# Second attention of a two-block kernel: the order of a step on TensorE and on VectorE

## The chip, the cores and the metric

The kernel runs on one core of one Trainium2 chip. The metric is the device time of one execution in microseconds (us). Before the change the median of three runs is 907.81 us (907.81 to 908.78). One further execution was profiled: 908.62 us, of which the profile's span, from the first instruction to the last, is 906.8 us.

## The reference, cut to what matters

The program computes a two-layer transformer block (a first attention layer, an MLP, a second attention layer, an MLP) and then a differential-attention layer, for 256 tokens of width 1024. Only the second attention layer bears on the change, and of it the two branches that attend over tokens. With 256 tokens all four 64-token blocks are kept and the window of 512 covers every earlier token, so both are causal softmax attentions over the same 256 keys, each with its own keys and values:

```python
s_s = jnp.einsum('bqghd,bgqkd->bghqk', qb, k_g) * scale
p_s = masked_softmax(s_s, valid_s[:, :, None]).astype(v_g.dtype)
o_s = jnp.einsum('bghqk,bgqkd->bqghd', p_s, v_g)
...
s_w = jnp.einsum('bqghd,bkgd->bghqk', qb, kw) * scale
p_w = masked_softmax(s_w, valid_w).astype(vw.dtype)
o_w = jnp.einsum('bghqk,bkgd->bqghd', p_w, vw)
out = gb[..., 0:1] * o_c + gb[..., 1:2] * o_s + gb[..., 2:3] * o_w
```

There are 16 heads in two groups of eight that share keys and values. The third branch (`o_c`, over 15 compressed keys) is computed for all heads at once, beside the steps described below.

## The kernel before

The kernel is written engine by engine: each engine has its own list of instructions, and counting semaphores order them. An engine does its list strictly in order, so an instruction that waits holds everything behind it on that engine.

The second attention is a software pipeline of 16 steps, one per head, counted by `it` from 0 to 18 (`STEPS_C = 16`, and `DEEP = 3` more to drain it). A step number `st` in the code is the head plus 8, since the eight steps of the first attention share the semaphores. For one head `n` the work is this, with the engine and the line that the profile shows:

- **Scores**, TensorE (`c_scores`, L1175): queries times both branches' keys. Token tile 0 goes to a bank of `pair`, tile 1 to a bank of `acc`; each has two banks, used by even and odd heads.
- **Maxima**, VectorE (`peaks`, L2000): four instructions add the causal mask, write the masked scores from PSUM to a buffer of `probs` in SBUF and leave the row maximum in `nb`. `probs` has three buffers (`DEEP`), so head `n` overwrites the buffer of head `n - 3`.
- **Exponentials**, ScalarE (`exponentials`, L1481): in place in `probs`, with the row sums. GpSimd makes of the sums the factors `cf` (L1893, L1913).
- **Two turns**, TensorE (`turn_p`, L974): turn 0 transposes the three 128x128 blocks of the first branch into the PSUM bank `ptp`, turn 1 those of the second branch into the same bank.
- **Two copies** out of `ptp`: the first on ScalarE (`p_first`, L1469), the second on VectorE (`p_second`, L2030).
- **Values**, TensorE (`mix`, L444): the transposed weights times the values, into `misc`. The program has six matmuls here; the trace shows each as two.
- **Scaling**, VectorE (`scaled`, L2036): `misc` times `cf` into `hr`; GpSimd adds the two branches into `o_tok` (L1918).

In iteration `it` the engines work on different heads: scores and maxima on head `it`, exponentials on head `it - 1`, the turns and copies on head `it - 3`, values and scaling on head `it - 4`. Before the change the order of an iteration is, for `it` from 4 to 15:

- TensorE: turn 0 of `it - 3`, scores of `it`, turn 1 of `it - 3`, values of `it - 4`.
- VectorE: copy of `it - 3`, maxima of `it`, scaling of `it - 4`. (For `it = 15` the maxima stand last.)
- ScalarE: copy of `it - 3`, exponentials of `it - 1`. This list is the same after the change.

The waits between them:

```python
def turn_p(st, a):                            # TensorE
    pe.wait_ge(s_exped, 2 * st + a + 1)
    pe.wait_ge(s_copied, 2 * st + a)
def mix(st, v):                               # TensorE
    pe.wait_ge(s_copied, 2 * st + 2)
    pe.wait_ge(s_scaled, st)
def peaks(st):                                # VectorE
    dve.wait_ge(s_turned, 2 * (st - DEEP + 1))
    dve.wait_ge(s_scored, 2 * st + t + 1)
```

Each turn adds one to `s_turned`, each copy one to `s_copied`. So a turn waits for the copy of the turn in front of it (one bank), the values of a head wait for its second copy, and the maxima of head `it` wait for turn 1 of head `it - 3`, whose buffer they overwrite.

Some iterations carry more, between the pieces named: on TensorE the scores against the compressed keys (`compressed_scores`, L1186 and L1191, at 3, 4, 7, 8), turns of query blocks (L417, at 3 and 5), a turn of the compressed weights (L1229, at 14); from 16 on the first turns of the output (`turn_outputs`, L1239 and L1243). On VectorE a weight split (L463, at 5, 8, 14), low halves of queries (L2278, at 4 and 6) and the softmax of the compressed branch (L2404 to L2417, from 7 to 13).

Of the kernel before, what the change touches and what calls it, by code (L numbers as in the profile page):

```python
# [90 lines left out]
def left(g):  # L91

    return g - min(max(g - G_ABO, 0), 2) - min(max(g - G_CO, 0), 2)
# [10 lines left out]
DEEP = 3  # L104
# [100 lines left out]
def program(nc, x, stream, consts_d, cols_d, rows_d, sel_d, out):  # L205
    with ExitStack() as ctx:  # L206
# [232 lines left out]
        def pe_pv(dst, src, v, w):  # L439

            for t, k0, nk in TK:
                for s in range(nk // P):
                    a = k0 + s * P
                    last = nc.tensor.matmul(dst[:, t * w:(t + 1) * w], src[:, a:a + P], v(s),  # L444
                                            start=s == 0, stop=s == nk // P - 1, skip_group_check=True)
            return last
# [231 lines left out]
        STEPS_AB = A_HEADS // 2 + B_HEADS // 2  # L678
        FOX = B_HEADS // 2
        STEPS_C = C_HEADS  # L680
# [3 lines left out]
        def c_q(st, n=1):  # L684

            tile, at_ = ((xh, KD + 4), (xl, KD + 4), (xh, 0), (xh, 4))[st // 4]
            return tile[:, at_ + st % 4:at_ + st % 4 + n, :]

        def c_keys(g, part):

            return (xh, xl)[part][:, KD + 2 * g:KD + 2 * g + 2, :]
# [9 lines left out]
        def c_q_bank(z):  # L701

            return (pair[Z_C % 2], pair[(Z_C + 1) % 2], acc[3], acc[3])[z]
# [15 lines left out]
        def c_bank(st, t):  # L719

            return (pair, acc)[t][st % 2][:, 0:2 * (t + 1) * P]

        def c_pt(st, a):

            return (pt, pt2)[st % 2][:, a, :]
# [48 lines left out]
        def _(pe):  # L774
# [193 lines left out]
            def turn_p(st, a):  # L968

                pe.wait_ge(s_exped, 2 * st + a + 1)  # L970
                pe.wait_ge(s_copied, 2 * st + a)
                pb = probs[:, st % DEEP, :]
                for k, c0 in enumerate((a * P, 2 * P + a * SEQ, 3 * P + a * SEQ)):
                    last = nc.tensor.transpose(ptp[:, k * P:(k + 1) * P], pb[:, c0:c0 + P], ident)  # L974
                last.then_inc(s_turned, 1)

            def mix(st, v):

                pe.wait_ge(s_copied, 2 * st + 2)
                if st >= 1:  # L980
                    pe.wait_ge(s_scaled, st)
                for a in range(2):
                    last = pe_pv(misc[:, a * P:(a + 1) * P], c_pt(st, a), v(a), HD)
                last.then_inc(s_mixed, 1)
# [182 lines left out]
            def c_scores(n):  # L1167

                st = STEPS_AB + n
                if st >= 2:  # L1170
                    pe.wait_ge(s_peaked, 2 * (st - 1))
                banks = [c_bank(st, t).rearrange("p (a k) -> p a k", a=2) for t in range(T)]
                for t in range(T):
                    for part in range(2):
                        last = mm(banks[t], c_q(n)[:, 0, t * P:(t + 1) * P], c_keys(n % CG, part)[:, :, 0:(t + 1) * P],  # L1175
                                  start=part == 0, stop=part == 1, skip_group_check=True)
                    last.then_inc(s_scored, 1)

            def c_values(n):

                return lambda a: lambda s: Y[:, s, (CVS, CVW)[a] + HD * (n % CG):(CVS, CVW)[a] + HD * (n % CG + 1)]
# [13 lines left out]

            def c_iter(it):

                if 0 <= it - DEEP < STEPS_C:
                    turn_p(STEPS_AB + it - DEEP, 0)
                if it < STEPS_C:  # L1200
                    c_scores(it)
                if it == 8:
                    compressed_scores(range(12, 16))
                if it >= STEPS_C:
                    mix(STEPS_AB + it - DEEP - 1, c_values(it - DEEP - 1))
                if 0 <= it - DEEP < STEPS_C:
                    turn_p(STEPS_AB + it - DEEP, 1)
                if DEEP < it < STEPS_C:
                    mix(STEPS_AB + it - DEEP - 1, c_values(it - DEEP - 1))
                if it == 3:  # L1210
                    pe.wait_ge(dve_prep, 10)
                    pe.wait_ge(ev_act, left(G_CO))
                    pe.wait_ge(ev_dve, left(G_CO))
                    compressed_scores(range(0, 4))
                if it == 4:
                    compressed_scores(range(4, 8))
                if it == 7:
                    pe.wait_ge(q_lo, 12)
                    compressed_scores(range(8, 12))
                if it in (3, 5):  # L1220
                    z = (it + 1) // 2
                    pe.wait_ge(q_roped, 6)
                    if z == 3:
                        pe.wait_ge(q_lo, 10)
                    pe_turn_z(pe, Z_C + z + 1, c_blocks[2 * z + 2:2 * z + 4], c_q_bank(z))
                if it == 14:
                    pe.wait_ge(dve_prep, 11)
                    for k in range(4):
                        last = nc.tensor.transpose(acc[3][:, k * P:(k + 1) * P], pc[:, k * P:(k + 1) * P], ident)  # L1229
                    last.then_inc(pe_prep, 1)  # L1230
# [739 lines left out]
        def _(dve):  # L1970
# [32 lines left out]
            def peaks(st):  # L2003

                dve.wait_ge(s_turned, 2 * (st - DEEP + 1))
                for t in range(T):
                    dve.wait_ge(s_scored, 2 * st + t + 1)
                    n = (t + 1) * P
                    for a in range(2):
                        last = masked_peak(st, a, t, c_bank(st, t)[:, a * n:(a + 1) * n], caus)  # L2010
                    last.then_inc(s_peaked, 1)
# [13 lines left out]
            def p_second(st):  # L2025

                dve.wait_ge(s_turned, 2 * st + 2)
                if st >= 2:
                    dve.wait_ge(s_mixed, st - 1)
                v_.tensor_copy(c_pt(st, 1), ptp[:, 0:KEYS]).then_inc(s_copied, 1)  # L2030
# [345 lines left out]
            def c_scaled(st):  # L2376

                if st >= 2:
                    dve.wait_ge(c_added, st - 1)
                scaled(STEPS_AB + st, c_mix(st), cf)  # L2380

            for it in range(STEPS_C + DEEP):
                if 0 <= it - DEEP < STEPS_C:
                    p_second(STEPS_AB + it - DEEP)
                if it < STEPS_C - 1:
                    peaks(STEPS_AB + it)
                if it > DEEP:
                    c_scaled(it - DEEP - 1)
                if it == STEPS_C - 1:
                    peaks(STEPS_AB + it)  # L2390
                if it in CO_SPLITS:
                    split(U_CO + CO_SPLITS.index(it))
                if it in (STEPS_C, STEPS_C + 1):
                    dve_turn_block(dve, 4, ccs=(it - STEPS_C,))
                if it == 1:
                    evac(dve, G_C + 3, U_CQ2 + 4, 1, Y[:, 1, CQ + GW:CQ + 2 * GW], rr(N_A1), GW)
                if it in (4, 6):
                    q_low(it // 2, Z_C + it // 2 + 1, 4 + it)
                if it in (7, 9):
                    b = it // 9  # L2400
                    dve.wait_ge(cmp_scored, b + 1)
                    parts = acc[2 + b][:, :].rearrange("p (t h a n) -> p t h n a", t=T, h=HPG, a=2)
                    for t in range(T):
                        v_.tensor_reduce(pc5[:, t, b], parts[:, t], AX.X, ALU.add).then_inc(parts_added, 1)  # L2404
                if it == 10:
                    dve.wait_ge(parts_added, 2 * T)
                    ch.link(v_.tensor_reduce(cmx, pcall, AX.X, ALU.max))
                    ch.link(v_.tensor_scalar(cmx, cmx, FLOOR, None, ALU.max))
                    v_.tensor_tensor(pcall, pcall, over_keys, ALU.subtract).then_inc(dve_mid, 1)
                if it == 12:  # L2410
                    dve.wait_ge(act_prep, 5)
                    ch.link(v_.tensor_reduce(cmx, pcall, AX.X, ALU.add))
                    ch.link(v_.tensor_scalar(cmx, cmx, 1e-30, None, ALU.max))
                if it == 13:
                    ch.link(v_.reciprocal(cmx, cmx))
                    ch.link(v_.tensor_tensor(cm3, cm3, gate_t[:, :, 0, :], ALU.mult))
                    v_.tensor_tensor(pcall, pcall, over_keys, ALU.mult).then_inc(dve_prep, 1)  # L2417
                if it == 15:
                    dve.wait_ge(pe_prep, 5)
                    v_.tensor_copy(pct[:, :], acc[3][:, :]).then_inc(dve_prep, 1)  # L2420
# [273 lines left out]
```

## Time and profile before

| | us |
|---|---|
| median of three runs | 907.81 (907.81 to 908.78) |
| the profiled execution, its own time | 908.62 |
| its span | 906.8 |
| TensorE busy | 890.7 (98%) |
| VectorE busy | 645.2 (71%) |
| ScalarE busy | 510.1 (56%) |
| GpSimd busy | 124.5 (14%) |

The second attention's steps lie between 369.9 and 433 us of the span, where the first scores and the last values are. Times in the rows below are microseconds from the span's start. PE is TensorE, PEld its weight loads, DVE VectorE, ACT ScalarE, POOL GpSimd. In a timeline a row is a group of equal instructions: its start, the time from the first one's start to the last one's end, engine, line, operation, output and input, and in brackets how long the engine stood idle before it and what released it. Matmuls overlap, so the next group may start before a row's time is over; what a group takes on the engine is read from start to start.

### The profile page before, as it was taken

How to read it: one execution, taken by the hardware profiler on the slowest of the kernel's cores; microseconds unless marked ns; L12 is line 12 of the kernel's file. 1: busy time of each engine (PE TensorE's matmuls, PEld its weight loads, DVE VectorE, ACT ScalarE, POOL GpSimd, SP SyncE). 2: the span in 40 equal slices, each digit the busy share in tenths (PEclk: the TensorE clock that was granted, in tenths of full speed). 3: DMA queues.
4: the chain of work that ended last, by engine and by line, in shares of the span. 5: the costliest groups of instructions: out<-in, count | busy, mean ns of one | idle time of the engine just before them, and what ended most of it. 6: DMA issues, size and time to landing. Idle time of an engine off the chain costs nothing. (4 is left out here: it accounts for less than half of the span.)

```text
span 906.8 us, 14857 instructions
## 1 busy us (share of the span) xinstructions
PE 890.7 (98%) x4796; PEld 745.2 (82%) x4796; DVE 645.2 (71%) x1305; ACT 510.1 (56%) x1017; POOL 124.5 (14%) x168
## 2 busy tenths in 40 slices
PE   8999999999999999999999999999999999999998
PEld 7878787888888888888878888888887778878876
DVE  4768756766666679687467666666876878777775
ACT  6654835444454466586354454444656666666573
POOL 1310300000000000354010000000430401400401
PEclk9999999999999999999999999999999999999999
DMA  9643143655555557010436565555464445454431
GB/s 343 225 158 98 46 144 123 210 198 191 191 194 193 190 178 247 33 47 25 140 116 217 196 192 192 195 191 188 141 223 145 140 140 182 147 182 141 162 117 47
DMA packets 41609, 145.75 MB, mean 161 GB/s; under 512 B 4688, under 2 KB 6224, under 8 KB 41552
## 3 DMA queue, kind: packets, MB, share of 16 engines
q1 hardware_dynamic: 41264, 144.93, 48.4%
q8 instruction: 34, 0.56, 0.3%
q14 instruction: 23, 0.19, 0.1%
q10 hardware_dynamic: 288, 0.07, 0.0%
HBM read 143.93 MB, written 1.05 MB: 160 GB/s over the span
## 5 line engine op out<-in xcount | busy, mean ns | idle before, releaser
L463 DVE TENSOR_TENSOR wl<-raw,wh 128x1024 fp32r<-128x1024 f32 (+2 forms) x270 | 329.1, 1222 | 88.7 <-ACT wh L458 86.2
L458 ACT ACTIVATE wh<-raw 128x1024 fp32r<-128x1024 f32 (+2 forms) x270 | 281.6, 1046 | 64.9 <-PE acc L355 43.4
L353 PE MATMUL acc<-wh,xhl 128*128 128x512 f32 (+1 forms) x472 | 190.7, 404 | 0.6 <-DVE xhl L2490 0.4
L355 PE MATMUL acc<-wh,xhl 128*128 128x512 f32 (+1 forms) x472 | 184.4, 391 | 0.0
L354 PE MATMUL acc<-wl,xhl 128*128 128x512 f32 (+1 forms) x472 | 183.9, 390 | 0.0
L353 PEld LDWEIGHTS acc<-wh,xhl 128*128 128x128 f32 x472 | 88.7, 188 | 25.0 <-issue 8.0
L355 PEld LDWEIGHTS acc<-wh,xhl 128*128 128x128 f32 x472 | 88.6, 188 | 19.2
L354 PEld LDWEIGHTS acc<-wl,xhl 128*128 128x128 f32 x472 | 88.8, 188 | 16.3
L353 PE MATMUL acc<-wh,hh 128*128 128x512 f32 x256 | 100.2, 391 | 0.0
L354 PE MATMUL acc<-wl,hh 128*128 128x512 f32 x256 | 100.0, 391 | 0.0
L355 PE MATMUL acc<-wh,hl 128*128 128x512 f32 x256 | 99.6, 389 | 0.0
L1507 ACT ACTIVATE hh<-hq 128x256 fp32r<-128x256 f32 x64 | 26.7, 418 | 77.3 <-PE acc L355 72.5
L815 PE MATMUL ptp<-xhl,wh 128*128 128x512 f32 x256 | 64.1, 390 | 1.1 <-DVE hr L2062 1.1
L1501 ACT ACTIVATE probs<-ptp 128x256 f32<-128x256 f32 x32 | 12.3, 383 | 93.7 <-PE ptp L822 93.7
L815 PE MATMUL misc<-xhl,wh 128*128 128x512 f32 x256 | 64.3, 391 | 0.7 <-DVE hr L2062 0.7
L2062 DVE TENSOR_TENSOR hr<-ptp,probs 128x256 f32<-128x256 f32 x32 | 13.6, 424 | 67.5 <-ACT probs L1501 67.5
L507 POOL TENSOR_SCALAR st<-st 128x2 f32<-128x2 f32 x7 | 2.4, 338 | 430.8 <-ACT o_tok L500 258.2
L815 PEld LDWEIGHTS misc<-xhl,wh 128*128 128x128 f32 x256 | 47.8, 188 | 11.2 <-DVE wl L463 1.5
L815 PEld LDWEIGHTS ptp<-xhl,wh 128*128 128x128 f32 x256 | 47.8, 188 | 11.2 <-issue 1.4
L355 PEld LDWEIGHTS acc<-wh,hl 128*128 128x128 f32 x256 | 48.1, 188 | 10.2
L353 PEld LDWEIGHTS acc<-wh,hh 128*128 128x128 f32 x256 | 48.2, 188 | 9.3
L354 PEld LDWEIGHTS acc<-wl,hh 128*128 128x128 f32 x256 | 48.2, 188 | 8.7
(302 smaller groups left out, 1355.2 us busy)
## 6 DMA issues: line engine op xcount, KB each, us to landing
raw<-stream SPq DMA_DIRECT2D x266, 512.0 KB, 3.4
raw<-stream SPq DMA_DIRECT2D x4, 352.0 KB, 5.7
h<-x SPq DMA_DIRECT2D x4, 256.0 KB, 4.0
out<-h SPq DMA_DIRECT2D x3, 256.0 KB, 2.1
row<-rows SPq DMA_DIRECT2D x1, 700.0 KB, 8.8
probs<-sel SPq DMA_DIRECT2D x1, 512.0 KB, 7.7
cst<-consts SPq DMA_DIRECT2D x1, 507.0 KB, 7.1
out<-h SPq DMA_DIRECT2D x2, 128.0 KB, 2.0
```

The source lines that it names most:

```text
L353: nc.tensor.matmul(out_, ah, bh, start=start, stop=False, skip_group_check=True)
L354: nc.tensor.matmul(out_, ah, bl, start=False, stop=False, skip_group_check=True)
L355: return nc.tensor.matmul(out_, al, bh, start=False, stop=stop_, skip_group_check=True)
L458: nc.scalar.activation(used(u, wh[:, u % SPLIT, :]), used(u, raw[:, u % RAW, :]), ACT.Copy).then_inc(w_hi, 1)
L463: nc.vector.tensor_tensor(used(u, wl[:, u % SPLIT, :]), used(u, raw[:, u % RAW, :]), used(u, wh[:, u % SPLIT, :]).bitcast(F32), ALU.subtra ...
L507: chain_link(nc.gpsimd.tensor_scalar(dst, src, 1.0 / width, EPS, ALU.mult, ALU.add))
L815: nc.tensor.matmul((ptp, misc)[f % 2][:, :], wh[:, u % SPLIT, k * P:(k + 1) * P], xhl[:, KD + k, :, :].rearrange("p a s -> p (a s)"), star ...
L1501: s_.activation(probs[:, f % 2, 0:SEQ], (ptp, misc)[f % 2][:, SEQ:2 * SEQ], ACT.Copy).then_inc(z_cross, 1)
L1507: s_.activation(hh[:, f % 2, :], hq[:, f % 2, :], ACT.Copy).then_inc(hid_hi, 1)
L2062: v_.tensor_tensor(hr[:, f % 2, :], bank[:, 0:SEQ], probs[:, f % 2, 0:SEQ], ALU.add).then_inc(z_summed, 1)
```

## The change

On TensorE the order of an iteration becomes scores of `it`, turn 0 of `it - 3`, values of `it - 4`, turn 1 of `it - 3`. On VectorE it becomes maxima of `it`, scaling of `it - 4`, copy of `it - 3`. No instruction is added or removed, and every wait stays on its instruction.

```diff
@@ c_iter(it), TensorE
-                if 0 <= it - DEEP < STEPS_C:
-                    turn_p(STEPS_AB + it - DEEP, 0)
+                if it == DEEP:
+                    turn_p(STEPS_AB, 0)
                 if it < STEPS_C:
                     c_scores(it)
+                if DEEP < it < STEPS_C + DEEP:
+                    turn_p(STEPS_AB + it - DEEP, 0)
                 if it == 8:
                     compressed_scores(range(12, 16))
-                if it >= STEPS_C:
+                if it > DEEP:
                     mix(STEPS_AB + it - DEEP - 1, c_values(it - DEEP - 1))
                 if 0 <= it - DEEP < STEPS_C:
                     turn_p(STEPS_AB + it - DEEP, 1)
-                if DEEP < it < STEPS_C:
-                    mix(STEPS_AB + it - DEEP - 1, c_values(it - DEEP - 1))
@@ loop over it, VectorE
-                if 0 <= it - DEEP < STEPS_C:
-                    p_second(STEPS_AB + it - DEEP)
-                if it < STEPS_C - 1:
+                if it < STEPS_C:
                     peaks(STEPS_AB + it)
                 if it > DEEP:
                     c_scaled(it - DEEP - 1)
-                if it == STEPS_C - 1:
-                    peaks(STEPS_AB + it)
+                if 0 <= it - DEEP < STEPS_C:
+                    p_second(STEPS_AB + it - DEEP)
```

TensorE, iteration 6, before the change (the semaphores that an instruction waits on stand in brackets; the rows without brackets are the rest of the same group):

```order
L974 MATMUL ptp<-cst,probs 128x128 [waits s_copied,s_exped]
L974 MATMUL ptp<-cst,probs 128x128 x2
L1175 MATMUL pair<-xhl 128x256 [waits s_peaked]
L1175 MATMUL pair<-xhl 128x256
L1175 MATMUL acc<-xhl 128x512 x2
L974 MATMUL ptp<-cst,probs 128x128 [waits s_copied,s_exped]
L974 MATMUL ptp<-cst,probs 128x128 x2
L444 MATMUL misc<-Y,pt 128x64 [waits s_scaled,s_copied]
L444 MATMUL misc<-Y,pt 128x64 x5
```

The same iteration after the change:

```order
L1175 MATMUL pair<-xhl 128x256 [waits s_peaked]
L1175 MATMUL pair<-xhl 128x256
L1175 MATMUL acc<-xhl 128x512 x2
L974 MATMUL ptp<-cst,probs 128x128 [waits s_copied,s_exped]
L974 MATMUL ptp<-cst,probs 128x128 x2
L444 MATMUL misc<-Y,pt 128x64 [waits s_scaled,s_copied]
L444 MATMUL misc<-Y,pt 128x64 x5
L974 MATMUL ptp<-cst,probs 128x128 [waits s_copied,s_exped]
L974 MATMUL ptp<-cst,probs 128x128 x2
```

The values have moved between the two turns, and the scores, which stood between them, in front. Between turn 1 of one iteration and turn 0 of the next there stood the values; now the scores stand there.

VectorE, iteration 10, before the change (the second instruction of each maximum, which stores `nb`, is listed by itself):

```order
L2030 COPY pt2<-ptp 128x384 [waits s_mixed,s_turned]
L2000 ISA probs,nb<-pair0,cst 128x128 [waits s_scored,s_turned]
L2000 ISA nb 128x1
L2000 ISA probs,nb<-pair0,cst 128x128
L2000 ISA nb 128x1
L2000 ISA probs,nb<-acc0,cst 128x256 [waits s_scored]
L2000 ISA nb 128x1
L2000 ISA probs,nb<-acc0,cst 128x256
L2000 ISA nb 128x1
L2036 TENSOR_TENSOR hr<-misc,cf 128x256 [waits s_coef,s_mixed,c_added]
L2407 TENSOR_REDUCE sml<-va 128x32 [waits parts_added]
```

After the change (the last row is the same reduction, two lines further up in the file):

```order
L2000 ISA probs,nb<-pair0,cst 128x128 [waits s_scored,s_turned]
L2000 ISA nb 128x1
L2000 ISA probs,nb<-pair0,cst 128x128
L2000 ISA nb 128x1
L2000 ISA probs,nb<-acc0,cst 128x256 [waits s_scored]
L2000 ISA nb 128x1
L2000 ISA probs,nb<-acc0,cst 128x256
L2000 ISA nb 128x1
L2036 TENSOR_TENSOR hr<-misc,cf 128x256 [waits s_coef,s_mixed,c_added]
L2030 COPY pt2<-ptp 128x384 [waits s_mixed,s_turned]
L2405 TENSOR_REDUCE sml<-va 128x32 [waits parts_added]
```

The copy has gone from the first place to the place behind the scaling. The first maximum keeps its wait on `s_turned`.

## Rows read from the trace of the kernel before

**Rows 1.** The page: the span, and the first of its busy times.

```profile
span 906.8 us, 14857 instructions
PE 890.7 (98%) x4796; PEld 745.2 (82%) x4796; DVE 645.2 (71%) x1305; ACT 510.1 (56%) x1017; POOL 124.5 (14%) x168
```

**Rows 2.** Windows: length, busy PE, PEld, DVE, ACT, POOL, then granted clock, DMA share.

```profile
400.00:410.00 10.00, 9.85 (x80) 8.63 (x79) 9.48 (x42) 8.47 (x34) 5.83 (x10) 1.00 0.17 54
410.00:420.00 10.00, 9.80 (x78) 8.42 (x78) 9.57 (x38) 8.09 (x30) 6.82 (x10) 1.00 0.05 6
```

**Rows 3.** Timeline, PE, iteration 10 and the turn that opens iteration 11.

```profile
401.34 0.50 PE L974 MATMUL ptp<-cst,probs 128*128 128x128 f32 x3
401.59 0.48 PE L1175 MATMUL pair<-xhl 128*128 128x256 f32 x2
...
402.51 0.52 PE L974 MATMUL ptp<-cst,probs 128*128 128x128 f32 x3
402.86 1.45 PE L444 MATMUL misc<-Y,pt 128*128 128x64 f32 x12
404.15 0.50 PE L974 MATMUL ptp<-cst,probs 128*128 128x128 f32 x3
```

**Rows 4.** Timeline, PE, iteration 8: scores, compressed scores, turn 1.

```profile
395.26 0.48 PE L1175 MATMUL pair<-xhl 128*128 128x256 f32 x2
...
396.04 0.96 PE L1191 MATMUL acc<-kcs,xhl 128*128 128x32 f32 x8
396.85 0.55 PE L974 MATMUL ptp<-cst,probs 128*128 128x128 f32 x3
```

**Rows 5.** Timeline, ACT, iteration 10: the first copy.

```profile
401.87 0.49 ACT L1469 ACTIVATE pt<-ptp 128x384 f32<-128x384 f32 x1 [0.58 <-PE ptp L974]
```

**Rows 6.** Timeline, DVE, iteration 10: copy, first maximum, scaling, the next instruction.

```profile
403.06 0.56 DVE L2030 COPY pt<-ptp 128x384 f32<-128x384 f32 x1
403.54 0.28 DVE L2000 CUSTOM_DVE_ANT_0 probs<-pair,cst 128x128 f32<-128x128 f32 x1
...
404.64 0.42 DVE L2036 TENSOR_TENSOR hr<-misc,cf 128x256 f32<-128x256 f32 x1
404.98 0.68 DVE L2407 TENSOR_REDUCE sml<-va 128x32 f32<-128x512 f32 x1
```

**Rows 7.** Timeline, PE, scores of head 1.

```profile
373.30 0.40 PE L1175 MATMUL pair<-xhl 128*128 128x256 f32 x2
```

**Rows 8.** Timeline, DVE, the first maximum of head 1.

```profile
373.84 0.29 DVE L2000 CUSTOM_DVE_ANT_0 probs<-pair,cst 128x128 f32<-128x128 f32 x1 [2.23 <-PE pair L1175]
```

**Rows 9.** Timeline, PE, first attention: a turn 1 and the next turn 0.

```profile
94.53 0.55 PE L974 MATMUL ptp<-cst,probs 128*128 128x128 f32 x3
95.82 0.52 PE L974 MATMUL ptp<-cst,probs 128*128 128x128 f32 x3 [0.74 <-DVE pt L2030]
```

**Rows 10.** Timeline, DVE, first attention: the copy between those two turns.

```profile
95.11 0.56 DVE L2030 COPY pt<-ptp 128x384 f32<-128x384 f32 x1 [0.61 <-PE ptp L974]
```

**Rows 11.** Timeline, PE: iteration 4 (turn 0, turn 1, what follows), and turn 1 of iteration 16.

```profile
379.61 0.85 PE L974 MATMUL ptp<-cst,probs 128*128 128x128 f32 x3
...
381.54 0.84 PE L974 MATMUL ptp<-cst,probs 128*128 128x128 f32 x3
...
383.60 1.04 PE L1191 MATMUL acc<-kcs,xhl 128*128 128x32 f32 x8
...
421.16 0.49 PE L974 MATMUL ptp<-cst,probs 128*128 128x128 f32 x3
```

**Rows 12.** Windows of 2 us, columns as in rows 2.

```profile
94.00:96.00 2.00, 1.26 (x13) 0.72 (x10) 1.39 (x8) 2.00 (x9) 0.95 (x1) 1.00 0.00 0
...
376.00:378.00 2.00, 1.28 (x13) 1.25 (x12) 1.48 (x8) 2.00 (x10) 1.74 (x5) 1.00 0.02 4
378.00:380.00 2.00, 1.34 (x8) 1.24 (x9) 1.00 (x8) 0.39 (x2) 1.92 (x4) 0.78 0.01 4
380.00:382.00 2.00, 2.00 (x10) 1.70 (x9) 0.00 (x0) 1.51 (x6) 1.24 (x3) 0.50 0.00 0
```

## The prediction

> **What bounds the kernel now.** I read the page first: TensorE is busy 890.7 of 906.8 us [rows 1], so the kernel is as long as TensorE's list, and a stage gets longer or shorter as TensorE waits more or less in it. Next come the windows of the stage that the change touches. In the two windows shown, from 400 to 420 us, TensorE is busy 9.85 and 9.80 of 10 us, but VectorE 9.48 and 9.57 [rows 2]: two engines are nearly full here, and an order that suits one may not suit the other. Last come the timelines of one iteration.
>
> On TensorE iteration 10 runs from 401.34 to 404.15, that is 2.81 us [rows 3]: turn 0 takes 0.25 until the scores start, 0.92 pass until turn 1, turn 1 takes 0.35, the values 1.29. The scores alone take 0.78, as iteration 8 shows where nothing makes the next piece wait (395.26 to 396.04) [rows 4]. So 0.14 us of the 2.81 is a wait: turn 1 needs the bank that ScalarE's copy empties from 401.87 to 402.36 [rows 5], and 0.15 later it starts. That wait is what the new order takes away: the values (1.29) then stand between the two turns.
>
> On VectorE the same iteration is copy, maxima, scaling: the copy starts at 403.06, 0.04 after turn 1 has ended (402.51 + 0.52, rows 3), the maxima start 0.48 later, the scaling 1.10 after them, and what follows 0.34 later [rows 6]. The copy (0.56) ends at 403.62, and turn 0 of the next iteration wants the bank at 404.15: it is hidden behind the values.
>
> **The change part by part.** *Turn 1 behind the values.* Saves the 0.14 us wait, once an iteration. In ten to twelve iterations that is at most 1.7 us, if nothing else waits.
>
> *The copy behind maxima and scaling.* This decides. The maxima of head `it` wait until turn 1 of head `it - 3` has read the buffer that they overwrite. Turn 1 is now the last piece of TensorE's iteration, so the maxima can't start earlier, though their scores are long there. Behind the waiting maxima, on VectorE's list, stand the scaling and the copy, and turn 0 of the next iteration waits for the copy. TensorE has only the next scores, 0.78 us, to put into that time. The loop from one turn 1 to the next, link by link:
>
> 1. turn 1, first transpose to last result: 0.50, as the turn behind the values at 404.15 [rows 3];
> 2. from there to the first maximum: 0.14. The trace has no maximum that a turn released; the copy starts 0.04 after a turn [rows 3, 6], a maximum that waits for scores 0.14 after them (373.30 + 0.40 = 373.70, then 373.84) [rows 7, 8]. I take the second, since it is the same instruction; 0.04 stays as the lower end;
> 3. four maxima: 1.10 [rows 6];
> 4. scaling: 0.34 until the next instruction starts [rows 6];
> 5. the copy: 0.56 [rows 6];
> 6. from its end to turn 0: 0.15. The first attention shows this link bare: copy from 95.11, over at 95.67 [rows 10], turn 0 at 95.82 after 0.74 idle [rows 9];
> 7. turn 0 until the values start: 0.35, as turn 1 before the values now [rows 3];
> 8. the values until turn 1: 1.29 [rows 3].
>
> Sum: 4.43 us for an iteration that takes 2.81 now. The scores, at 0.26 to 1.04 us of the loop, lie inside links 1 to 5 and cost nothing; so do ScalarE's copy (over 0.5 us after turn 0's end, while the values run) and what VectorE does behind its copy (at most a split or a piece of the softmax: it has links 6 to 8 and the next turn, 2.3 us). GpSimd's factors and sums are as far from their users as before.
>
> *How many loops.* From turn 1 of iteration 4 to turn 1 of iteration 16 there are 12. Now these lie at 381.54 and 421.16 [rows 11], 39.62 us. After the change the first comes later, because the values have moved in front of it: turn 0, scores, turn 1 and values of iteration 4 fill TensorE from 379.61 to 383.60 without a gap, and in the new order turn 1 is the last of the four. It took 0.26 to 0.63 of that stretch (at the clock's two levels), so it starts at about 383.2. Twelve loops are 53.2 us. One extra piece lies on the loop, the compressed scores of iteration 8, which stand between turn 0 and the values: 0.81 (396.04 to 396.85) [rows 4]. The other extra pieces of TensorE (iterations 4, 5, 7, 14) stand behind turn 1, at most 1.0 us each, and fit into the wait there, which is 1.7 us long. So turn 1 of iteration 16 comes at 383.2 + 53.2 + 0.8 = 437.2 instead of 421.16: **16.0 us later**.
>
> *Before and behind.* Iteration 3 keeps its order on TensorE; VectorE's copy there comes 1.1 us later, before a turn 0 that is more than 2 us away. From iteration 16 on TensorE's order is as before, and the pieces from there on (the output turns and the weights' matmuls, which bind on TensorE) shift as a whole. DMA is nearly idle in the stage (shares 0.17 and 0.05) [rows 2], so nothing is late that would have been in time.
>
> Sum for the profiled execution: 906.8 + 16.0 = 922.8 of span, with the 1.8 us around it 924.6. It lay 0.8 above the median of its runs, so I predict a median of **923.8 us**.
>
> *A rule weighed against the trace.* Both turns use one bank, and the trace shows a turn waiting for the copy out of it [rows 9]. The Trainium skill's page "Perfetto Trace Analysis", section "Matmuls", says that independent matmul groups should rotate through different PSUM banks, so that emptying one overlaps the next group. By that rule the loss would be one of the bank, and a second bank would give it back. By the rows it would not: the values need the same copy as the turn does, so a loop with two banks still has every link but number 7 (4.08 instead of 4.43), and 12 of them save only 4.2 us of the 16.
>
> **The rivals.** *The clock falls.* TensorE would work 2.7 us of 4.43 and stand still for 1.7. The trace has one stretch in which the granted clock falls to the lower level (1.2 GHz): TensorE is busy 1.28 and 1.34 us of 2 us, much of it with small matmuls, then the clock is 0.78 and 0.50 [rows 12], and a turn takes 0.85 instead of 0.50 [rows 11, 3]. Another stretch as thin, 1.26 of 2 us, keeps 1.00 [rows 12]. At the lower level link 1 costs 0.35 more, link 7 about as much, link 8 up to 1.29 more: 2.0 us a loop. For half of the loops that is 12 more, 936; for all of them 948. What speaks against it is that the idle time is cut by 1.3 us of dense matmuls in every loop, and that at the lower level TensorE would be nearly full again, after which the trace shows the clock rise. The Trainium skill has a rule for this case: "TensorE: Matmul & The Clock Gate", section "A second HAM failure mode: psum-queue depth-cycling", tells of a kernel whose frequent short idle times between groups made the clock swing between its levels. By that rule the time is the 936 of this rival; of the two thin stretches here one agrees with it and one doesn't.
>
> *TensorE keeps its pace, faster.* No turn waits, and an iteration is TensorE's own work, 0.78 + 0.35 + 1.29 + 0.26 = 2.68 us. Against 2.81 twelve of them save 1.6 us: 906.2. The place where this is decided is turn 0 behind the scores. TensorE gets there 0.26 + 0.78 = 1.04 after turn 1 began, and VectorE's answer to that turn must be in the bank by then, 0.54 after the turn's end. By links 2 to 6 it takes 2.29. Nothing in the rows speaks for it but that VectorE had finished its maxima before the turn in every iteration of the old order. That the change does not do what it says is ruled out by the listings.
>
> *The maxima run ahead, no change.* If the wait on the turn let the maxima pass, because I misread its count, they and the scaling would be done when turn 1 ends, and the copy would start at once. Then the loop is 0.50 + 0.04 + 0.56 + 0.15 + 0.35 + 1.29 = 2.89, beside 2.81 now: 12 x 0.08 is 1 us more, less what of TensorE's extra pieces fits into the short wait. That is no change that can be measured. The order's listing shows the wait on `s_turned` at the first maximum, and three buffers leave no other count.
>
> **How the numbers follow.** My forecast, 922 to 926, has a chance of 0.70: the lower end is link 2 at 0.04 (12 x 0.10 less) and turn 1 of iteration 4 a little earlier. The clock's rival has 0.22, spread from 926 to 948, around 936. TensorE's own pace has 0.02, the maxima that run ahead 0.03, and 0.03 are for a link that I misread. The range of 8 in 10 leaves out the last three and the upper half of the clock's: 921.0 to 934.0. Differences below 0.2% (1.8 us) a measurement of this kernel can't tell from none. Faster by more: 0.02; within: 0.03; slower by more: 0.95.
>
> **What would show it.** In the profile after: TensorE idle for about 1.7 us before turn 0 of iterations 6 to 15 (less where an extra piece stands behind turn 1), released by VectorE's copy; turns 1 of neighbouring iterations 4.4 us apart; each group of maxima idle before it and released by a turn instead of by scores; the stage from first scores to last values 16 us longer, and everything behind it unchanged in length. The granted clock in the stage tells the first rival: 1.00 throughout but for the one stretch near 380. I am wrong if turns 1 lie less than 4 us apart at full clock, or if the maxima start before turn 1 has ended.

## The result and the profile after

The changed kernel takes **937.76 us**, median of 6 runs (933.29 to 939.75). The kernel before, run beside it, takes 908.13 (6 runs, 907.81 to 909.59). The ratio is 1.0319, with an interval of 1.0301 to 1.0336. The forecast was 923.8, its range 921.0 to 934.0: the sign was right, the size was not. The profiled execution took 938.4 us.

The page after (the span, the first busy times, TensorE's clock in 40 slices):

```profile
span 936.6 us, 14857 instructions
...
PE 907.9 (97%) x4796; PEld 760.3 (81%) x4796; DVE 645.4 (69%) x1305; ACT 510.0 (54%) x1017; POOL 123.0 (13%) x168
...
PEclk9999999999999999956999999999999999999999
```

The span is 29.8 us longer than before [rows 1], but TensorE is idle only 12.6 us more. It is *busy* 17.2 us more with the same 4796 matmuls. So matmuls have become slower, and the clock's row says where: two slices in the middle, at 5 and 6 tenths. The windows of that stage (columns as in rows 2):

```profile
390.00:394.00 4.00, 2.84 (x22) 2.44 (x22) 2.81 (x10) 2.87 (x11) 2.35 (x4) 1.00 0.23 66
394.00:398.00 4.00, 2.75 (x23) 2.78 (x23) 3.06 (x11) 3.00 (x11) 1.43 (x3) 0.91 0.18 68
398.00:402.00 4.00, 4.00 (x19) 3.70 (x18) 2.09 (x8) 0.79 (x4) 1.62 (x3) 0.50 0.00 0
...
414.00:418.00 4.00, 3.64 (x19) 3.67 (x19) 0.88 (x3) 2.24 (x9) 0.70 (x2) 0.50 0.00 0
...
434.00:438.00 4.00, 4.00 (x18) 3.34 (x17) 1.08 (x7) 1.96 (x9) 1.22 (x2) 0.50 0.00 0
438.00:442.00 4.00, 3.00 (x27) 2.88 (x26) 2.82 (x12) 2.38 (x10) 0.53 (x2) 0.97 0.00 0
...
446.00:450.00 4.00, 2.29 (x15) 2.32 (x16) 2.16 (x9) 1.92 (x10) 1.63 (x3) 0.81 0.28 105
```

At full clock TensorE is busy 2.8 of 4 us. Near 397.3 the clock falls to the lower level, and it stays there until about 438.2: one stretch of about 41 us in which the same iterations keep TensorE busy 3.1 to 4.0 us of 4. From 448.5 to 451.9 it is down once more, behind the wait of iteration 16. (A short stretch near 380 is in both profiles, before [rows 12] and after.) Now the timeline of TensorE, one loop on either side of the fall (start, duration, work, idle time before it and what ended it):

```profile
392.57 0.50 PE L974 MATMUL ptp<-cst,probs 128*128 128x128 f32 x3
...
395.25 0.52 PE L974 MATMUL ptp<-cst,probs 128*128 128x128 f32 x3 [1.48 <-DVE pt L2030]
395.61 1.45 PE L444 MATMUL misc<-Y,pt 128*128 128x64 f32 x12
396.89 0.50 PE L974 MATMUL ptp<-cst,probs 128*128 128x128 f32 x3
...
411.33 0.85 PE L974 MATMUL ptp<-cst,probs 128*128 128x128 f32 x3
...
414.36 0.87 PE L974 MATMUL ptp<-cst,probs 128*128 128x128 f32 x3 [0.91 <-DVE pt L2030]
415.03 2.66 PE L444 MATMUL misc<-Y,pt 128*128 128x64 f32 x12
417.48 0.85 PE L974 MATMUL ptp<-cst,probs 128*128 128x128 f32 x3
...
447.71 0.52 PE L974 MATMUL ptp<-cst,probs 128*128 128x128 f32 x3 [2.18 <-DVE pt L2030]
448.06 2.27 PE L444 MATMUL misc<-Y,pt 128*128 128x64 f32 x12
```

From turn 1 to turn 1 it is 4.32 us at full clock and 6.15 at the lower level, against 2.81 before [rows 3]. VectorE between the turns at 392.57 and 395.25 (first maximum, scaling, copy):

```profile
393.11 0.29 DVE L2000 CUSTOM_DVE_ANT_0 probs<-pair,cst 128x128 f32<-128x128 f32 x1 [1.19 <-PE ptp L974]
...
394.22 0.42 DVE L2036 TENSOR_TENSOR hr<-misc,cf 128x256 f32<-128x256 f32 x1
394.56 0.55 DVE L2030 COPY pt<-ptp 128x384 f32<-128x384 f32 x1
```

Every link stands there: the turn ends at 393.07 and the first maximum starts 0.04 later, released by the turn and no longer by the scores [rows 8]; maxima 1.11, scaling 0.34, copy 0.55, 0.14 to turn 0, 0.36 to the values, 1.28 to the next turn 1. The view of waits (waiter, releaser: us in total, times, longest) has the two halves of the loop as groups of their own:

```profile
DVE probs L2000 <- PE ptp L974: 33.3, 13, 6.0
...
PE ptp L974 <- DVE pt L2030: 13.3, 14, 2.2
```

**Where the time went.** Turn 1 of iteration 4 starts at 383.92 instead of 381.54, that is 2.38 later; turn 1 of iteration 16 at 450.13 instead of 421.16 [rows 11], that is 28.97 later. Between them the 12 loops take 66.21 instead of 39.62. Five of them, between 405.18 and 435.94, take 6.15, 1.83 too much each. The loop of iteration 8, with the compressed scores, takes 8.29 at the lower level, and 5.24 in a run at full clock (the scores issued twice, below). The loop of iteration 14, in which the clock came back, takes 4.76, and 4.42 in that same run. In the last loop the values take 2.07 instead of 1.28, because the clock has fallen again. That is 9.15 + 3.05 + 0.34 + 0.79 = 13.3 for the clock. The rest, 28.97 - 13.3 = 15.6, is the chain of waits and its start. Behind turn 1 of iteration 16 another 0.83 goes to the same second fall: the next turn 0 follows after 2.95 us instead of 2.12. So of the 29.8 us of the span, 15.6 are the chain and 14.2 the clock. The forecast had 16.0 for the chain, and nothing for the clock.

### The profile page after: what moved, and what is told of

The parts are those of the page before. It is cut to its first block and busy times, and to the rows that moved or that the text cites. A ratio compares the mean times of both kernels' runs of the same rounds, so it can differ in the third digit from the quotient of the medians.

```text
span 936.6 us, 14857 instructions
## 1 busy us (share of the span) xinstructions
PE 907.9 (97%) x4796; PEld 760.3 (81%) x4796; DVE 645.4 (69%) x1305; ACT 510.0 (54%) x1017; POOL 123.0 (13%) x168
```

## The experiments

The loss may be the chain alone, the chain and a clock that falls because of it, or something else in the new order of TensorE. The first seven were chosen to part these. In the diffs, lines with + and - stand against the changed kernel, unless another is named.

**The scores three times, and twice.** The scores of heads 5 to 15 are issued again in place (the same values, to the same banks). That fills the idle time before turn 0 with matmuls and leaves every wait as it is.

```diff
                 for t in range(T):
+                    for _ in range(2 if n > DEEP + 1 else 0):
+                        for part in range(2):
+                            mm(banks[t], ..., start=part == 0, stop=part == 1, skip_group_check=True)
                     for part in range(2):
```

> The changed order, with the scores of heads 5 to 15 computed three times in place (the first two results are overwritten by the same numbers), so that TensorE has 1.56 us more work in each wait behind turn 1. Theory (the chain through VectorE costs about 16 us, TensorE's lower clock the other 13 to 14): the work fits into the wait, the granted clock stays at 1.00 after the stretch near 380, turns 1 lie 4.3 us apart, and the time falls to 922 to 926. Rival (the clock has no part, what is slow is TensorE's own list): 11 heads x 1.56 us come on top, about 955. Rival (all of the loss is clock, the chain is hidden): about 908.

With the `2` as `1`:

> The changed order, with the scores of heads 5 to 15 computed twice in place (the first result is overwritten by the same numbers): 0.78 us more work in each wait, which leaves TensorE about 0.9 us idle in each loop. If the idle time is what lets the clock fall, and it falls by degrees: part of the stage at the lower level, 928 to 935. If half the filling is enough: as with three times, 926 to 929. If the clock only holds when the wait is full: 936 to 940.

Measured: three times 927.71 us (925.77 to 928.79), ratio 1.0221 (1.0206 to 1.0236); twice 925.80 (924.38 to 926.03), 1.0186 (1.0171 to 1.0202). Windows of the kernel with the scores twice, the same stretch:

```profile
406.00:410.00 4.00, 3.22 (x27) 2.77 (x26) 2.34 (x12) 2.15 (x9) 1.47 (x3) 1.00 0.24 93
410.00:414.00 4.00, 3.22 (x26) 2.77 (x25) 3.14 (x10) 1.92 (x9) 1.63 (x3) 1.00 0.00 0
414.00:418.00 4.00, 3.23 (x25) 2.73 (x25) 1.79 (x10) 2.44 (x9) 1.62 (x3) 1.00 0.00 0
```

and its timeline:

```profile
413.26 0.50 PE L974 MATMUL ptp<-cst,probs 128*128 128x128 f32 x3
...
415.94 0.52 PE L974 MATMUL ptp<-cst,probs 128*128 128x128 f32 x3 [0.77 <-DVE pt L2034]
...
417.58 0.50 PE L974 MATMUL ptp<-cst,probs 128*128 128x128 f32 x3
```

TensorE has more to do in every loop, and the kernel is 10 to 12 us *faster*. The loop stays at 4.32 us, and in the profiled execution with the scores twice the clock is 1.00 until 433: the chain has nothing to do with the scores, and most of what the change costs beyond the chain is the clock. Only behind the wait of iteration 16, which has no scores to fill it (2.18 us, as in the change), does the clock still fall, from 433.1 to 439.6. At three times, turn 1 of iteration 16 starts at 437.43, where the prediction had put it at 437.2; that is close partly by chance, since some of these loops are longer than 4.32 (4.95, 4.49 and, at a fallen clock, 5.04).

**Small matmuls as filling.** Seven matmuls of 128x64 ahead of the scores of heads 5 to 15, into a bank that the scores then overwrite.

```diff
+                for k in range(7 if n > DEEP + 1 else 0):
+                    mm(c_bank(st, k % T)[:, 0:HD], ident, cst[:, C_TRI:C_TRI + HD], start=True, stop=True,
+                       skip_group_check=True)
                 for t in range(T):
```

> The changed order, with seven float32 matmuls of 64 columns in front of the scores of heads 5 to 15, into the scores' own bank (their results are overwritten), of the shape and type of the values' matmuls: as much time in the wait as two more sets of scores, 1.5 us. Theory (TensorE standing idle lets the clock fall): the clock holds, 925 to 929. Rival (it is not idle time as such; small matmuls don't hold the clock, as the values did not bring it back in the profile after the change): the clock falls although TensorE is hardly idle, 936 or more, since the filling is then also twice as long (3 us) and no longer fits.

Measured: 928.24 (927.64 to 929.36), ratio 1.0216 (1.0200 to 1.0231). The granted clock is 1.00 from 386 to 434 us, the plain loops are 4.32. The rival of 936 or more is not borne out: matmuls as small as the values serve here about as well as the large ones of the same length (927.71 with the scores three times).

**VectorE: scaling, copy, maxima.** TensorE keeps the new order; on VectorE the maxima, which wait for turn 1, go behind the copy.

```diff
-                if it < STEPS_C:
-                    peaks(STEPS_AB + it)
                 if it > DEEP:
                     c_scaled(it - DEEP - 1)
                 if 0 <= it - DEEP < STEPS_C:
                     p_second(STEPS_AB + it - DEEP)
+                if it < STEPS_C:
+                    peaks(STEPS_AB + it)
```

> TensorE in the changed order, VectorE in the order scaling, copy, maxima. Theory: the copy then answers turn 1 at once (0.04 + 0.56 + 0.15 us after its end), the loop is 0.50 + 0.04 + 0.56 + 0.15 + 0.35 + 1.29 = 2.89 us, the clock stays up, and the time is 907 to 909, as before the change. Rival (TensorE's new order is itself the loss): 920 or more.

Measured: 909.10 (908.47 to 911.23, 11 runs), ratio 1.0012 (1.0003 to 1.0021). Its timeline on TensorE:

```profile
401.79 0.50 PE L974 MATMUL ptp<-cst,probs 128*128 128x128 f32 x3
...
403.20 0.52 PE L974 MATMUL ptp<-cst,probs 128*128 128x128 f32 x3 [0.20 <-DVE pt L2030]
403.56 1.45 PE L444 MATMUL misc<-Y,pt 128*128 128x64 f32 x12
```

and on VectorE:

```profile
402.17 0.42 DVE L2036 TENSOR_TENSOR hr<-misc,cf 128x256 f32<-128x256 f32 x1
402.50 0.55 DVE L2030 COPY pt<-ptp 128x384 f32<-128x384 f32 x1
402.97 0.28 DVE L2000 CUSTOM_DVE_ANT_0 probs<-pair,cst 128x128 f32<-128x128 f32 x1
```

In the loop shown the copy starts 0.21 after turn 1 has ended, and turn 0 waits 0.20 instead of 1.48. With this order on VectorE, TensorE's new order costs a thousandth; with the changed order the loss is the place of scaling and copy behind the waiting maxima.

**VectorE's new order alone.** Against the kernel before: TensorE as it was, VectorE maxima, scaling, copy (VectorE's half of the diff above the prediction).

> TensorE in its order before the change, VectorE in the changed order (maxima, scaling, copy). Theory (the place of the copy behind the waiting maxima costs, whatever TensorE's order): the scaling now waits for values that come behind turn 1, so the copy lands 2.9 us after turn 1 begins, and with turn 0, scores and the wait for ScalarE's copy (1.2) the loop is 4.1 us; about 10 us more than before the change at full clock, 916 to 920, more if the clock falls as it did with both orders changed. Rival (it takes both orders together): 907 to 909.

Measured: 922.11 (919.47 to 927.23, 4 runs), ratio 1.0159 (1.0125 to 1.0193). TensorE:

```profile
389.54 0.52 PE L974 MATMUL ptp<-cst,probs 128*128 128x128 f32 x3
389.90 1.45 PE L444 MATMUL misc<-Y,pt 128*128 128x64 f32 x12
392.48 0.52 PE L974 MATMUL ptp<-cst,probs 128*128 128x128 f32 x3 [1.13 <-DVE pt L2030]
...
393.67 0.52 PE L974 MATMUL ptp<-cst,probs 128*128 128x128 f32 x3
```

The loop is the expected one, 4.13 us from turn 0 to turn 0, and the one run at a clock of 1.000 took 919.47, inside the expectation; the median lies some 2 us above it. So it does not take both orders: VectorE's order costs 1.6% with TensorE's old order too. VectorE's copy still stands behind maxima and scaling: the maxima start at 390.10, 0.04 after turn 1, and the scaling at 391.44, when the values have ended too; the copy follows at 391.78 and ends at 392.33. In the profiled execution the clock fell twice in this stage (near 405.7 and 419.6), each time for a few us.

**VectorE: copy, maxima, scaling, with TensorE's new order** (VectorE's lines of the kernel before).

```diff
+                if 0 <= it - DEEP < STEPS_C:
+                    p_second(STEPS_AB + it - DEEP)
-                if it < STEPS_C:
+                if it < STEPS_C - 1:
                     peaks(STEPS_AB + it)
...
-                if 0 <= it - DEEP < STEPS_C:
-                    p_second(STEPS_AB + it - DEEP)
+                if it == STEPS_C - 1:
+                    peaks(STEPS_AB + it)
```

> TensorE in the changed order, VectorE in its order before the change: copy, maxima, scaling. Theory: turn 0 gets its bank early, but the values wait for the scaling, which now stands behind copy and maxima: 0.50 + 0.04 + 0.48 + 1.10 + 0.42 + 0.15 + 1.29 = 3.98 us a loop, about 10 us in all, 918 at full clock; TensorE would idle 1.3 us of 3.98, and if the clock falls for most of the loops (5.5 us each) up to 936. Rival (only the place of the copy on VectorE matters): 907 to 909.

Measured: 920.04 (917.19 to 922.39), ratio 1.0133 (1.0112 to 1.0155). TensorE:

```profile
408.76 0.50 PE L974 MATMUL ptp<-cst,probs 128*128 128x128 f32 x3
...
411.44 1.52 PE L444 MATMUL misc<-Y,pt 128*128 128x64 f32 x12 [0.92 <-DVE hr L2036]
412.80 0.50 PE L974 MATMUL ptp<-cst,probs 128*128 128x128 f32 x3
```

A loop of 4.04, closed by another wait: the values need `misc`, which the scaling empties, and now the scaling stands behind copy and maxima. At a clock of 1.000 a run took 917.19, near the 918 expected. So TensorE's new order with VectorE's old one loses 1.3%: each half of the change costs by itself, this one by another wait. Of the three orders run on VectorE with TensorE's new one, only the one with the maxima last costs next to nothing.

**A fourth buffer.** Both new orders stay; every fourth head gets a fourth buffer (in `work` and `ka`; the code that picks it is not shown), so the maxima wait for a turn that lies one iteration further back.

```diff
+BUFS = 4
-                dve.wait_ge(s_turned, 2 * (st - DEEP + 1))
+                dve.wait_ge(s_turned, 2 * max(st - BUFS + 1, STEPS_AB))
```

> Both lists as changed, but a fourth buffer for the masked scores in the second attention, so that the maxima wait for a turn 1 that lies an iteration further back. Theory (the wait of the maxima on turn 1 is what puts maxima and scaling ahead of the copy): maxima and scaling are done before turn 1 ends, the loop is 2.89 us, the time 907 to 909. Rival (the copy behind maxima and scaling is late by VectorE's work alone, about 9.5 of 10 us busy, whatever the maxima wait for): 915 or more.

Measured: 913.32 (910.08 to 913.95), ratio 1.0053 (1.0039 to 1.0067): between the two expectations. Most of the loss is gone, with the bank `ptp` still single. What is left, on TensorE:

```profile
408.58 0.52 PE L985 MATMUL ptp<-cst,probs 128*128 128x128 f32 x3 [0.60 <-DVE pt L2040]
...
410.22 0.50 PE L985 MATMUL ptp<-cst,probs 128*128 128x128 f32 x3
411.51 0.52 PE L985 MATMUL ptp<-cst,probs 128*128 128x128 f32 x3
...
413.15 0.50 PE L985 MATMUL ptp<-cst,probs 128*128 128x128 f32 x3
```

The best loops take 2.93 (410.22 to 413.15). In others the maxima start late because VectorE is still busy with the compressed branch's softmax, and the copy behind them is late without any wait on a turn. So the wait on the buffer carried most of the loss, and the copy's place behind the maxima keeps a smaller price of its own. Part of that is again the clock: the one run at 1.000 took 910.08, and in the profiled execution the clock fell for 3.4 us behind a wait of 1.80 in iteration 16.

**Values between the turns.** Against the kernel before: the first values matmul of a head moves between the scores and turn 1, to cover the 0.14 us that turn 1 waits for its bank (`mix` takes the part as a third argument; that code is not shown).

```diff
+                if DEEP < it < STEPS_C:
+                    mix(STEPS_AB + it - DEEP - 1, c_values(it - DEEP - 1), 0)
                 if 0 <= it - DEEP < STEPS_C:
                     turn_p(STEPS_AB + it - DEEP, 1)
                 if DEEP < it < STEPS_C:
-                    mix(STEPS_AB + it - DEEP - 1, c_values(it - DEEP - 1))
+                    mix(STEPS_AB + it - DEEP - 1, c_values(it - DEEP - 1), 1)
```

> The kernel before the change with one of the six matmuls of the values moved between scores and turn 1. Theory (at full clock an iteration is TensorE's own work plus the 0.14 us wait of turn 1 for ScalarE's copy): the wait goes, the other five matmuls (1.07 us) still cover VectorE's copy, an iteration takes 2.68 instead of 2.81, and the time falls by 1 to 2 us to 906 to 907. Rival (the wait comes back in front of turn 0, or VectorE, 9.5 of 10 us busy, is the bound already): no change.

Measured: 908.05 (907.72 to 909.85, 11 runs), ratio 1.0005 (0.9996 to 1.0014). TensorE:

```profile
401.00 0.41 PE L983 MATMUL misc<-Y,pt 128*128 128x64 f32 x2 [0.20 <-DVE hr L2045]
401.24 0.50 PE L974 MATMUL ptp<-cst,probs 128*128 128x128 f32 x3
```

Turn 1 no longer waits; in some iterations the moved matmul does, for the scaling. The gain of 1 to 2 us did not come; the rival, no change, was right. No version of the study beats the kernel before.

**Where the filling matters.** Scores twice for heads 9 to 15 alone (`n > 8`), and for heads 5 to 8 alone (`DEEP + 1 < n < 9`).

> The changed order; the scores of heads 9 to 15 are issued twice in place (same values, same banks), those of heads 5 to 8 once. Tests the sentence of the prediction that TensorE, nearly full at the lower level, gets its clock back. In the changed kernel the clock fell at about 396.8, between the scores of heads 7 and 8. If a TensorE without idle time gets it back: the same fall, then at the lower level the doubled scores (0.78 us more at full clock, 1.57 at the lower) fill the 0.9 us of idle time, the clock is 1.00 again by about 405, loops from there are 4.32, and the time is that of the scores issued twice everywhere plus 2 to 7 us: 927 to 933. If it stays low once it has fallen, whatever TensorE does: loops of 6.15 - 0.90 + 1.57 = 6.8 us, 5 or 6 of them, that is 3 to 4 us more than the changed kernel: 939 to 943.

> The changed order; the scores of heads 5 to 8 are issued twice, those of heads 9 to 15 once. If it is the idle time of each loop that takes the clock down, wherever it stands, the clock falls later, in iterations 10 to 12, and fewer loops are slow: 6.15 - 4.32 = 1.83 us for each loop behind the fall, 3 to 6 of them: 929 to 937. If it is one place, around iterations 7 and 8 (where the compressed scores and the small matmul stand), nothing falls later: loops of 4.32 throughout, 924 to 927.

Measured: filled from 9 on, 926.61 (922.10 to 930.06), ratio 1.0183 (1.0136 to 1.0230); filled up to 8, 930.58 (927.60 to 933.14), ratio 1.0237 (1.0195 to 1.0279). Windows of the kernel filled up to head 8:

```profile
398.00:402.00 4.00, 3.86 (x32) 3.38 (x30) 1.40 (x9) 3.18 (x10) 1.35 (x2) 1.00 0.00 0
402.00:406.00 4.00, 2.67 (x22) 2.44 (x22) 2.83 (x12) 2.11 (x9) 0.66 (x3) 1.00 0.13 20
406.00:410.00 4.00, 2.52 (x20) 2.37 (x19) 2.17 (x10) 1.91 (x10) 1.62 (x3) 0.90 0.29 111
410.00:414.00 4.00, 3.10 (x14) 2.41 (x13) 3.47 (x13) 1.13 (x5) 1.68 (x3) 0.50 0.01 4
...
426.00:430.00 4.00, 3.89 (x17) 3.24 (x16) 1.19 (x9) 1.86 (x9) 1.22 (x2) 0.54 0.00 0
430.00:434.00 4.00, 3.04 (x26) 2.88 (x26) 2.81 (x14) 2.48 (x10) 0.61 (x2) 1.00 0.00 0
```

The clock falls here too, but near 409 instead of 397, behind the first two loops that wait the full 1.48, and three loops of 6.15 follow, as the first expectation had it. With the scores twice in all heads it did not fall in the loops at all. So it is the idle time of the loops that takes it down, not the compressed scores of iterations 7 and 8.

In the profiled execution filled from 9 on, the clock fell earlier, near 379.6, as in the kernel before [rows 12], and was back before the filled iterations began:

```profile
382.00:386.00 4.00, 4.00 (x22) 4.00 (x21) 1.33 (x9) 2.88 (x11) 1.21 (x2) 0.50 0.00 0
386.00:390.00 4.00, 4.00 (x18) 3.70 (x19) 2.04 (x4) 1.71 (x8) 0.46 (x1) 0.50 0.02 4
390.00:394.00 4.00, 3.95 (x20) 3.26 (x19) 2.61 (x11) 1.48 (x4) 1.68 (x3) 0.55 0.00 0
394.00:398.00 4.00, 2.52 (x21) 2.11 (x20) 2.79 (x12) 3.31 (x11) 1.50 (x3) 1.00 0.39 131
```

The fall at 397 that it was to undo did not happen in that execution. So the question whether a TensorE without idle time would have raised a clock that had fallen inside the loops is not answered by it. It gives something else: its four runs had mean granted clocks of 1.000, 0.998, 0.991 and 0.989, at 922.10, 924.17, 929.04 and 930.06 us, that is 0.72 us for each thousandth. The 922.10 is the new order with no clock lost, in one run, 14.9 us above the kernel before at a clock of 1.000 (907.16 and 907.24 beside it).

## Why the prediction was right and wrong

**The mechanism held.** All eight links were found where the prediction put them, 4.32 us against 4.43: the difference is link 2, which is 0.04, the end that the prediction kept as its lower one and did not take. TensorE's wait is 1.48 and not 1.7, because the scores last 0.94 to their last result and not 0.78; the loop does not depend on that. The scores cost nothing: in the plain loops they could be doubled and tripled within the same 4.32. The chain cost 15.6 us in the profile after, where the sum had 16.0, and 14.9 in the one run with no clock lost (922.10, inside the 922 to 926 of the forecast). That the sum is this good is partly luck: the loops began 0.7 later than predicted, and at full clock they would have been 1.1 shorter.

**The single bank was not most of the loss.** The rule of the Trainium skill's "Perfetto Trace Analysis", section "Matmuls", that independent groups should rotate through PSUM banks, would have blamed the single bank. The fourth buffer left the bank single and took the ratio from 1.0319 to 1.0053, and VectorE's order scaling, copy, maxima took it to 1.0012. A second bank was not tried, so the 4.2 us that the prediction gave it stay untested.

**The step that failed** is the weighing of the clock: the sum had no term for it, and the measured one is 14.2 us. The prediction had the rival and nearly its price: 2.0 us a loop, measured 6.15 - 4.32 = 1.83 (0.35 on links 1 to 6, 0.31 on link 7, 1.17 on link 8). It gave it 0.22 because "the idle time is cut by 1.3 us of dense matmuls in every loop, and that at the lower level TensorE would be nearly full again, after which the trace shows the clock rise". Both halves were wrong. The values between the waits did not keep the clock up: it fell after loops of just that kind, here near 397.3 and in the kernel filled up to head 8 near 409. And a TensorE that was nearly full, or full, did not bring it back soon: after the fall it worked for 10 us without a pause, to 407.30, at a clock of 0.50; then it waited 0.90 us of each 6.15, and the clock stayed down for 41 us in all. The range left out the upper half of this rival, and 937.76 lies there.

The Trainium skill's "TensorE: Matmul & The Clock Gate", section "A second HAM failure mode: psum-queue depth-cycling", tells of a clock that swings between its levels under frequent short idle times. The trace agrees in the fall, behind waits of up to 1.48 us, but not in the swinging: within the loops the clock fell once and stayed at 0.50 for 41 us. The 936 of the rival came within 2 us of the median, partly by chance: it stood for six slow loops of 2.0 us each, and there were five of 1.83 and 5.0 us of other losses beside them.

**The start of the loops** came a little later than predicted: turn 1 of iteration 4 at 383.92 instead of 383.2. Nor was everything behind the stage unchanged in length: the second fall of the clock added 0.83 us there.

## What to carry to other kernels

When a piece that waits is put ahead of another on an in-order engine, follow what stands behind it until the loop closes, and add up the links: that sum was good to 3% here. Then ask what the new idle time does to TensorE's clock, because a loop that waits can cost twice, here 15.6 us in the waits and 14.2 in matmuls at about half speed. If the wait can't be removed, filling it with work that is thrown away can pay: here doubled scores gave back 12 of 30 us.

## What was not expected of the hardware

Loops that differ in how long TensorE waits in each (two of the kernels differ in their order too), the mean granted clock of whole executions (all runs of each kernel), and what the clock did inside the loops of the one profiled execution:

| kernel | idle us in a full-clock loop | loop us | granted clock of its runs | falls inside the loops |
|---|---|---|---|---|
| scores twice | 0.78 | 4.32 | 0.996 to 0.998 | none |
| copy, maxima, scaling | 0.92 | 4.04 | 0.994 to 1.000 | none |
| VectorE's order alone | 1.13 | 4.13 | 0.991 to 1.000 | two, of 3.6 and 3.4 us |
| scores twice up to head 8 | 1.48 (from iteration 9) | 4.32 | 0.984 to 0.991 | one, of about 21 us |
| the change | 1.48 | 4.32 | 0.973 to 0.982 | one, of about 41 us |

The longer the wait in each loop, the more of the clock was lost, and all six runs of the change were low. The mean of a run also holds falls outside the loops, near 380 and from iteration 16 on, so small differences between the means say little. It does not always follow: filled from head 9 on, two loops that waited 1.48 and 0.47 passed at 1.00.

The wait in front of turn 0 of iteration 16 shows the same. It was 2.18 or 2.19 us in the six profiled executions with both new orders and three buffers, and 1.80 with four; in all seven the clock fell in it or within 2 us behind it. With scaling first, copy first, and VectorE's order alone it was 0.93, 0.74 and 1.25 us, and the clock stayed at 1.00.

What brings the clock back stays open. In the change TensorE was without a pause from 395.25 to 407.30; the clock fell in the midst of that stretch, near 397.3, and was still at the lower level at its end. It rose near 438.2, just behind the scores, in an iteration that looked like the four before it. In the kernel filled up to head 8 it rose near 429.7, about 21 us after it fell, again with the same 0.90 us waits on the way. Filled from head 9 on, it rose 14 us after the fall near 379.6, with TensorE busy all but 0.05 us of the time from 382 to 394. With VectorE's order alone it was back within 4 us, twice. A prediction for such a loop should therefore hold both cases wide, rather than argue one of them away.
